# Two heads' products with the values in one pair of column groups, scores kept in their bank, exponentials behind the copies

## What is computed

```
s_loc = where(valid, q . k_loc * scale + bias, -1e30);  s_ctx = q . k_ctx * scale
p = softmax(concat(s_loc, s_ctx))                      # 512 + 256 keys
out = p_loc . v_loc + p_ctx . v_ctx                    # neighbourhood attention
out = softmax((qn . kn + qr . kr) * 96 ** -0.5) . v    # latent attention, 256 + 512 keys
```

## Time and profile before

| | us |
|---|---|
| median of three runs | 5595.64 |
| the profiled execution, its own time | 5615.22 |
| its span, first to last instruction | 5613.4 |
| PE busy | 4447.6 (79%) |
| DVE busy | 3051.5 (54%) |
| ACT busy | 1241.3 (22%) |
| POOL busy | 2763.0 (49%) |
| PE busy with the products with the values (L835), 1664 matmuls | 217.8 |

### The profile page before, as it was taken

The page is one execution under the profiler, slowest core; times in us unless marked ns, Lnnn a source line. Parts: engine busy times, 40 slices in busy tenths (PEclk is TensorE's granted clock), DMA queues, the critical chain, the costliest instruction groups (busy, mean ns, idle before and its releaser), DMA issues.

```text
span 5613.4 us, 57357 instructions
## 1 busy us (share of the span) xinstructions
PE 4447.6 (79%) x19168; PEld 2455.9 (44%) x19168; DVE 3051.5 (54%) x8176; ACT 1241.3 (22%) x3643; POOL 2763.0 (49%) x2566
## 2 busy tenths in 40 slices
PE   7989798889997887997855558999788889655555
PEld 4467643433585344653411115558533455311111
DVE  0211767776217776556676542431677655777643
ACT  1321222333212321112211112540133211111111
POOL 0000466666304655666677770000366466777776
PEclk9889898888998888998977888999888999877778
DMA  5544799988747878999999992114688799999999
GB/s 189 189 153 142 282 367 340 335 311 331 253 137 279 324 286 304 379 398 358 356 390 369 394 389 83 55 39 154 221 310 318 278 366 399 391 391 391 362 403 353
DMA packets 464130, 1651.73 MB, mean 294 GB/s; under 512 B 51168, under 2 KB 57440, under 8 KB 463840
## 3 DMA queue, kind: packets, MB, share of 16 engines
q0 software_dynamic: 368640, 1342.34, 63.2%
q1 hardware_dynamic: 95200, 305.73, 15.2%
HBM read 1645.77 MB, written 2.10 MB: 294 GB/s over the span
## 4 chain that ended last, share of the span: by engine, by line
PE 50%; POOL 15%; DVE 13%; DMA 11%; issue 7%; ACT 3%; SPq 0%; DVEq 0%; POOLq 0%; ACTq 0%; PEldq 0%
PE banks L647 16%; PE banks L925 10%; DMA vb<-in_peer_v_dram,idx 8%; POOL vb L1446 8%; POOL ub L1435 7%; DVE ub L1386 5%; PE banks L736 4%; PE banks L663 3%; PE banks L773 3%; PE banks L835 3%; PE banks L812 2%; PE banks L758 2%; PE banks L823 1%; DMA ub<-in_peer_u_dram,idx 1%; PE banks L715 1%
## 5 line engine op out<-in xcount | busy, mean ns | idle before, releaser
L1435 POOL DMA_INDIRECT ub<-in_peer_u_dram,idx x1280 | 1424.1, 1113 | 2270.7 <-DVE idx L1374 1375.1
L925 PE MATMUL banks<-vb,dg 128*64 128x512 f32 x5120 | 1571.7, 741 | 695.7 <-DMA vb<-in_peer_v_dram,idx 626.4
L1386 DVE CUSTOM_DVE_ANT_0 ub<-ub,h2cur 128x1024 f32<-128x1024 f32 x1280 | 1529.6, 1223 | 611.1 <-DMA ub<-in_peer_u_dram,idx 485.9
L1446 POOL DMA_INDIRECT vb<-in_peer_v_dram,idx x1280 | 1338.3, 1046 | 561.0 <-issue 342.5
L925 PEld LDWEIGHTS banks<-vb,dg 128*64 128x64 f32 x5120 | 406.7, 160 | 1596.1 <-issue 1336.4
L647 PE MATMUL banks<-region,wring 128*128 128x256 f32 x3840 | 882.2, 390 | 35.8 <-ACT region L989 25.3
L647 PEld LDWEIGHTS banks<-region,wring 128*128 128x128 f32 x3840 | 738.7, 195 | 215.8 <-issue 104.9
L1135 ACT ACTIVATE dg<-consts,wgt 128x64 f32<-128x64 f32 x1280 | 358.4, 337 | 836.5 <-PE banks L925 425.3
L647 PE MATMUL banks<-h2T,wring 128*128 128x256 f32 x1280 | 316.9, 406 | 21.1 <-ACT h2T L989 21.1
L1329 DVE SCALAR_TENSOR_TENSOR region<-region,banks 128x256 f32<-128x256 f32 x120 | 50.5, 421 | 486.0 <-PE banks L647 485.9
L736 PE MATMUL banks<-region,wring 128*128 128x256 f32 (+1 forms) x1056 | 260.7, 404 | 48.0 <-ACT region L989 48.0
(11 more groups left out here) (146 smaller groups left out, 4004.9 us busy)
## 6 DMA issues: line engine op xcount, KB each, us to landing
wring<-w_gate_dram SPq DMA_DIRECT2D x120, 512.0 KB, 5.0
wring<-w_mod_dram SPq DMA_DIRECT2D x96, 512.0 KB, 4.6
wring<-w_pq_dram SPq DMA_DIRECT2D x80, 512.0 KB, 5.4
wring<-w_branch_dram SPq DMA_DIRECT2D x60, 512.0 KB, 3.6
wring<-w_out_dram SPq DMA_DIRECT2D x40, 512.0 KB, 4.7
ub<-in_peer_u_dram,idx POOLq DMA_INDIRECT x1280, 6.6
vb<-in_peer_v_dram,idx POOLq DMA_INDIRECT x1280, 6.6
region<-in_na_rpb_dram SPq DMA_DIRECT2D x64, 256.0 KB, 3.0
```

The source lines that it names most:

```text
L925: ins = nc.tensor.matmul(bank(ACC[a])[64 * g:64 * g + 64, :], dg[:, n % DG_RING, :], vb[:, n % V_RING, a * 512:(a + 1) * 512], start=first ...
L1386: nc.vector.tensor_tensor_reduce(out=ub[:, n % U_RING, :], in0=ub[:, n % U_RING, :], in1=h2cur[:, g, :], scale=1.0, scalar=0.0, op0=ALU.mu ...
L1435: pool.indirect_dma_start(ub[:, n % U_RING, :], None, u_rows, bass.IndirectOffsetOnAxis(ap=idx[:, u % IDX_RING, j:j + 1], axis=0)).then_in ...
L1446: pool.indirect_dma_start(vb[:, n % V_RING, :], None, v_rows, bass.IndirectOffsetOnAxis(ap=idx[:, u % IDX_RING, j:j + 1], axis=0)).then_in ...
```

## The change

Three edits. First, `mixv` takes two neighbouring units (two heads of a tile) in every second round, and writes them to the two halves of one bank, matmul by matmul in turn, at tile positions (0, 0) and (0, 64); one copy of 128 partitions takes both out. `pr` now has two slots and `ptr` three. Second, DVE writes the biased scores back into their own bank; ACT takes the exponentials from there, and frees it. Third, ACT's exponentials of unit i are a step of their own, `exp`, which stands behind the step `turn` of unit i-2.

```diff
-        pr = at3(E + 1024, 3, 768)
-        ptr = at3(E + 3328, 2, 768)
+        pr = at3(E + 1024, 2, 768)
+        ptr = at3(E + 2560, 3, 768)
...
                 if 2 <= i < n + 2:
                     emit(("turn", l, s, kind, i - 2))
-                if 3 <= i:
-                    emit(("mixv", l, s, kind, i - 3))
+                if i < n:
+                    emit(("exp", l, s, kind, i))
+                if i >= 4 and i % 2 == 0:
+                    emit(("mixv", l, s, kind, i - 4))
...
# PE
-                    emptied(pe, un["key"] + ("t", len(un["k"]) - 1))
-                    for j, vv in enumerate(un["v"]):
-                        ins = nc.tensor.matmul(bk[un["po"]:un["po"] + 64, 0:P], vv, ptr[:, i % 2, j * P:(j + 1) * P],
-                                               start=(j == 0), stop=(j == nv - 1))
+                    emptied(pe, two[1]["key"] + ("t", len(two[1]["k"]) - 1))
+                    for j in range(nv):
+                        for e, un in enumerate(two):
+                            ins = nc.tensor.matmul(bk[64 * e:64 * e + 64, 0:P], un["v"][j],
+                                                   ptr[:, (i + e) % 3, j * P:(j + 1) * P],
+                                                   start=(j == 0), stop=(j == nv - 1), tile_position=(0, 64 * e),
+                                                   skip_group_check=True)
...
# ACT
-                elif op == "score":
+                elif op == "exp":
...
-                    if i >= 3:
-                        whole(act, t_hist[-1])
...
-                        if a == 0 and un["bias"] is not None:
-                            nc.scalar.activation(dst, dst, ACT.Exp, bias=st[:, 2:3], scale=-1.0, accum_out=st[:, 4:5])
-                        else:
-                            bk = whole(act, key)
-                            ins = nc.scalar.activation(dst, bk[:, 0:w], ACT.Exp, bias=st[:, 2:3], accum_out=st[:, 4 + a:5 + a])
-                            frees(ins, key)
+                        bk = whole(act, key)
+                        sign = -1.0 if a == 0 and un["bias"] is not None else 1.0
+                        frees(nc.scalar.activation(pr[:, i % 2, off:off + w], bk[:, 0:w], ACT.Exp, bias=st[:, 2:3], scale=sign,
+                                                   accum_out=st[:, 4 + a:5 + a]), key)
...
-                    frees(nc.scalar.activation(un["dest"], bk[po:po + 64, 0:P], ACT.Copy), key)
+                    frees(nc.scalar.activation(un["dest"], bk[:, 0:P], ACT.Copy), key)
...
# DVE
-                        if i >= 3:
-                            whole(dve, t_hist[i - 3] + ("t", 1))
...
-                        frees(nc.vector.tensor_tensor_reduce(out=pr[:, i % 3, 0:512], in0=bk, in1=bias[:, nb % 2, :], scale=-1.0,
-                                                             scalar=st[:, 0:1], op0=ALU.add, op1=ALU.min,
-                                                             accum_out=st[:, 2:3]), key)
-                        emptied(dve, key)
-                        dve.sem_inc(neg_max, 1)
+                        nc.vector.tensor_tensor_reduce(out=bk, in0=bk, in1=bias[:, nb % 2, :], scale=-1.0, scalar=st[:, 0:1],
+                                                       op0=ALU.add, op1=ALU.min, accum_out=st[:, 2:3]).then_inc(neg_max, 1)
```

More of the change, by code:

```diff
@@ L434, in na_stage @@
                         un = dict(key=(l, s, "na", t, h), q=naq[s][rows, ch, t * P:(t + 1) * P], po=p0,
-                                  dest=aT[s][rows, ch, t * P:(t + 1) * P], bias=None)
+                                  dest=aT[s][:, ch, t * P:(t + 1) * P], bias=None)
                         if s:
@@ L488, in mla_stage @@
                                           v=[vm[:, a, cols] for a in range(nk // P)],
-                                          dest=mT[p0:p0 + 64, h // 2, t * P:(t + 1) * P]))
+                                          dest=mT[:, h // 2, t * P:(t + 1) * P]))
                 units_of[(l, s, ("mla", grp))] = units
@@ L822, in _ @@
                         for j in range(w // P):
-                            ins = nc.tensor.transpose(bk[:, j * P:(j + 1) * P], pr[:, i % 3, off + j * P:off + (j + 1) * P],
+                            ins = nc.tensor.transpose(bk[:, j * P:(j + 1) * P], pr[:, i % 2, off + j * P:off + (j + 1) * P],
                                                       ident)
@@ L828, in _ @@
                     _, l, s, kind, i = step
-                    un = units_of[(l, s, kind)][i]
-                    key = un["key"] + ("o",)
+                    two = units_of[(l, s, kind)][i:i + 2]
+                    key = two[0]["key"] + ("o",)
                     bk = fill(key)
-                    emptied(pe, un["key"] + ("t", len(un["k"]) - 1))
-                    nv = len(un["v"])
-                    for j, vv in enumerate(un["v"]):
-                        ins = nc.tensor.matmul(bk[un["po"]:un["po"] + 64, 0:P], vv, ptr[:, i % 2, j * P:(j + 1) * P],
-                                               start=(j == 0), stop=(j == nv - 1))
+                    emptied(pe, two[1]["key"] + ("t", len(two[1]["k"]) - 1))
+                    nv = len(two[0]["v"])
+                    for j in range(nv):
[4 more added lines that the diff above has]
+                                                   skip_group_check=True)
                     fills(ins, key)
@@ L942, in _ @@
             last_spread, last_tail = [None], [None]
-            t_hist, o_hist, sig_hist, mod_keys = [], [], [], []
+            sig_hist, mod_keys = [], []
             def link(ins):
@@ L1051, in _ @@
                     un = units_of[(l, s, kind)][i]
-                    if i >= 2:
-                        whole(act, o_hist[-1])
+                    if i >= 3:
+                        whole(act, units_of[(l, s, kind)][(i - 3) // 2 * 2]["key"] + ("o",))
                     off = 0
@@ L1057, in _ @@
                         bk = whole(act, key)
-                        frees(nc.scalar.activation(ptr[:, i % 2, off:off + w], bk[:, 0:w], ACT.Copy), key)
+                        frees(nc.scalar.activation(ptr[:, i % 3, off:off + w], bk[:, 0:w], ACT.Copy), key)
                         off += w
-                    t_hist.append(key)
                 elif op == "mixv":
@@ L1152, in _ @@
             cnt = dict(sc=0, bias=0, sgt=0, sigs=0, gexp=0, kt=0)
-            t_hist = []
             def link(ins):
@@ L1351, in _ @@
                     fence_wait(dve, step[1])
-                elif op == "turn":
-                    _, l, s, kind, i = step
-                    if i == 0:
-                        t_hist.clear()
-                    t_hist.append(units_of[(l, s, kind)][i]["key"])
                 elif op == "topk":
```

5 lines of the change are left out of this document (1 added, 4 removed).

## The result

| | before | after |
|---|---|---|
| median, us (8 executions each) | 5604.63 | 5644.03 |
| lowest to highest | 5584.25 to 5614.72 | 5625.51 to 5652.43 |
| profiled execution, its span | 5613.4 | 5630.5 |
| mean granted clock | 0.867 | 0.857 |

The ratio is 1.007, interval [1.0052, 1.0088]: 39 us more. A second comparison of the same pair gave 1.0054 [1.0034, 1.0074]. I had forecast 5601, no measurable change.

A forecast was written before the change was run, and what follows sets the result against it. PE was taken to bound stages without background; with background no engine was full and the plan's order decided. The terms -15 + 12 + 8 = +5 us on a 5595.6 median gave 5601 us, range 5580 to 5615 (8 in 10: 5560 to 5636).

The forecast's parts named there:

- -9: Context's first stage: 16 pairs of 256-key units save 11 us of PE, some hidden by weight loads; -9 us.
- +12 for the neighbourhood stage (between -8 and +29) and +8 for the three latent ones (0 to +26): Stages with background: exponentials, now behind background pieces and copies, delay scores and DVE; +12 and +8 us.
- the full PE gain of 8: First layer's neighbourhood stage, lower end: 0.24 us saved for each of 32 units, -8 us.
- exponentials behind DVE-fed pieces cost in full: Rival, four stages with background: ACT's late exponentials cost +29+26, less 15 is +40, 5636 us; chance 0.28.
- PE's clock falling in the stages without background: Sign of a wrong forecast, left out of the sum because gaps stay under 0.8 us.
- +1: Second layer's latent A, two groups of 8 units: waits outweigh the pairs' gain by 0.3 a group; +1 us.
- a wait of 1.75 in a group's third round: Latent groups: third round has turn and scores with nothing between in both kernels, and waits 1.75 us.
- -7: Second layer's neighbourhood stage: some 14 pairs keep 0.47 of 1.45 us each, -6.6, with its ends -7 us.
- the pair's product at 1.45 us: Product in column groups: 24 alternating matmuls plus one passage take 1.45 us for two units instead of 2.90.
- edit 2 and the bias DMA at nothing: Scores stored and read in their bank, and bias DMA waiting for the exponential: no cost, 6 us store allowance.
- The column groups do not overlap: Rival, paired products: with different inputs or by the skill's rule, -7 and -9 fall to about -1 each; 5620; chance 0.05.
- the idle time swallows the new waits: Rival, background stages: PE and DVE idle time absorbs late scores, giving lower ends, -29, 5567 us; chance 0.27.

The follow-up runs named there:

- mid_only: The kernel before with ACT's exponential moved behind the background's pieces of its round but ahead of the transposes' copies; 1.0053 of the kernel before.
- late_bg_last: The kernel before with the exponential behind the transposes' copies and the background's pieces moved to the end of the round; 0.9963 of the kernel before.
- after_bg_last: The kernel after with the background's pieces moved to the end of the round, behind the exponential; 5558.36 us, 0.9921 of the kernel before.
- pairs2: The kernel before with paired products only, after the transposes; ACT takes the product out before copying the next transposes; 0.9973 of the kernel before.
- bank_only: The kernel before with only biased scores stored back into their bank, which ACT's exponential reads and frees; 1.0000 of the kernel before.

## Why the prediction was wrong

What failed is one step under several terms: I took the time that pairs save on PE, and the price of each wait, at the clock of the kernel before. The clock did not stay: 0.63 instead of 0.86 in the window of the context's neighbourhood attention, 0.82 instead of 0.90 in the first layer's. The context's term had the wrong sign by it (-9, measured +12); why its clock stayed low is open. The terms with background came to +30 where I had +20, in the first stage with the clock's part in it; for the three latent stages (+11 instead of +8) I have no such split. A smaller part is the start of the sum: 5595.6 was the median of three runs, the median of eight is 5604.6, which makes 9 of the 43 us between 5601 and 5644.

- **"+12 for the neighbourhood stage (between -8 and +29) and +8 for the three latent ones (0 to +26)"** measured +19 and +11: 30 instead of 20. The mechanism is the one that I read from the earlier trace rows; `mid_only`, `late_bg_last` and `after_bg_last` confirm the place (ACT, behind pieces fed by DVE) and exclude the copies. In the first stage the exponential's place costs 17 us, well below my upper end of 29. But the full PE gain of 8, my lower end, isn't there: `pairs2` takes 278.8 against 276.5. I left out PE's clock. It went from 0.90 to 0.82; waits without pairs have 0.86 (`mid_only`), pairs without waits 0.85 (`pairs2`). The rival "exponentials behind DVE-fed pieces cost in full" came nearer to the time (5636), but partly by luck: of its 55 us 30 came, and the context's stages made up for the rest.
- **"-9" for the context's stages** measured +12, the largest error of all, 21 us. I took the matmuls saved at the granted clock of the window before. The latent part came (-3.2). In the neighbourhood part the clock stayed at 0.50 some 30 us longer. I named "PE's clock falling in the stages without background, which I leave out since gaps stay under 0.8 us": the clock was low here with no gaps at all.
- **"+1" for the second layer's latent A** measured -6.5. I counted a wait of 1.75 in a group's third round. The timeline of the kernel after has 0.55 there, and 0.55 once more in the next round:

```profile
3658.88 1.02 PE L814 MATMUL banks<-region 96*128 96x512 f32 x2
3660.45 0.70 PE L814 MATMUL banks<-region 96*128 96x256 f32 x2 [0.55 <-ACT region L1046]
```

  In the first rounds no product takes a bank, so the job five back is another one than in steady state. Each of two groups is 1.4 shorter (30.4 from the first scores to the last product, 31.8 before). About 3 us more are the profile of before itself: five kernels with single products took 150.7 to 152.2 in this stage, that profile 154.4.
- **"-7"** for the second layer's neighbourhood stage (-8.0), the pair's product at 1.45 us, and edit 2 and the bias DMA at nothing were right (DVE waits 0.6 us for a bias row in the first layer's neighbourhood stage, before and after). "The column groups do not overlap" is refuted, and so is "the idle time swallows the new waits": PE's 41.7 us of waits lengthened the stage.

So in the second layer's two stages without background the change brings what was worked out, or more; the pieces ahead of the exponential take back more than that, and the clock in one early stage some more.

## What to carry to other kernels

When an instruction is moved back on an in-order engine, list all that it now stands behind and ask who feeds each: here pieces that wait for a third engine cost 17 us of one stage, and copies that were ready nothing. If it must move, move the foreign pieces behind it as well; here that turned 0.5 to 0.7% slower into 0.8% faster. And a cheaper product isn't worth its matmul time before the granted clock of its stage has been read both before and after, in several executions: here PE was busy 11 us less in one stage that became no shorter.

## What the runs showed of the hardware

- Matmuls (128 rows, 64 columns of weights, 128 moving) that alternate between two column groups ran 24 in 1.53 us with different inputs and weights, where 12 in one group took 1.52.
- The granted clock can stay at 0.50 while PE is busy 20.00 of 20 us. How long it stays differs between executions of one kernel by 20 us and more (stage lengths of 66.1 to 88.7).
- After a stretch with PE busy 3.23 of 6 us the granted clock went from 1.00 to a mean of 0.66, and eight 128x512 matmuls took 3.62 instead of 1.94 us. Over a whole stage the same 1152 matmuls kept PE busy 239.2 us at a clock of 0.86 (`mid_only`) and 223.2 at 0.90 (`late_bg_last`).
- An exponential of 128x512 with its source in a bank takes 0.69 us and one from SBUF 0.72; a DVE instruction of that size that stores into a bank instead of SBUF 0.76 instead of 0.75, and its accumulator read 0.14 instead of 0.08. `bank_only`, with both, took as long as the kernel before (1.0000).
